# Block inverse of the recurrence in 32x32 tiles, and each direction's sequence over two periods with two chains interleaved

## The chip, the cores and the metric

One Trainium2 chip, one of its cores, float32 throughout. The metric is device time in microseconds (us) of the one launch. Before the change the median of three runs is 3419.12 us (3416.22 to 3426.52).

## The reference, cut to what matters

The program is one layer of a hybrid trunk for a context group (128 positions) and a latent group (512 positions), D = 2048. The change touches one of its parts, the bidirectional RWKV-7 recurrence: 16 heads of width 64, two directions, and per head a 64x64 state that is carried through all positions.

```
def wkv_scan(r, w, k, v, a, b, s0, reverse):
    def step(S, xs):
        r_t, w_t, k_t, v_t, a_t, b_t = xs
        sa = jnp.einsum('bhvk,bhk->bhv', S, a_t)
        S = S * w_t[:, :, None, :] + sa[..., None] * b_t[:, :, None, :] + v_t[..., None] * k_t[:, :, None, :]
        return S, jnp.einsum('bhvk,bhk->bhv', S, r_t)
...
for d, (s0, rev) in enumerate(((s0_f, False), (s0_b, True))):
    ...   # decay, a_rate, k_d of direction d
    o_d, s_d = wkv_scan(..., -kk, kk * a_h, s0, rev)
```

The outputs of both directions are added. Around it lie the input projection, attention, gating, the output projection and an expert layer, none of which changes.

## The kernel before, in words

`block_rwkv` (L1066 to L1590) handles a pair of heads at a time (`NPAIR` = 8, the two heads on partitions 0-63 and 64-127) and for each pair both directions `d`. That makes 16 *periods* (`u = 2p + d`). The 640 positions are `NCK` = 10 chunks of `CK` = 64, two of the context and eight latent.

Per period the kernel prepares one direction and at the same time runs the sequence of the direction prepared in the period before. Everything is written out by hand in a list, `timeline` (L1093 to L1101): 60 *jobs*, and between them the 30 *stages* of the sequence, about one stage after every two jobs. PE, ScalarE (ACT) and VectorE (DVE) each walk the same list in order; a semaphore wait holds all that stands behind it on its engine.

The jobs (`run_job`, L1299) write a rotating set of six PSUM banks (`rot`), and `empty` on ACT (L1406) or DVE (L1499) takes the result out:

- `bk` (3), `vt` (2): products with the identity that turn k, b and v to token order; emptied by ACT.
- `sc` (5): 64x64 by 128 products, two chunks in a job; DVE masks them (L1505).
- `w`, `a` (two halves each) and `s0`: decay and rate of the *next* direction, emptied by ACT with Sigmoid; then the scan on DVE (L1520), six vector operations on GpSimd (POOL; `front`, L1222, and `scaled_r`, L1239), three Exp on ACT (L1435 to L1437) and three products on DVE (L1529, L1534).
- `ti` (3), and then five levels of `x`, `dt`, `dtt` (three batches of 4, 3 and 3 chunks): the inverse of a 64x64 unit triangular matrix per chunk and head by doubling, from blocks of 1 to blocks of 64. POOL starts it (L1253, L1255). Level by level `x` multiplies by the triangular matrix `sc`, DVE masks (L1512), `dtt` and `dt` update the inverse `tt` and its transpose `tm` (L1515). Both are kept since a matmul takes its left side transposed.

All these matmuls go head by head through `heads` (L1286), as 64x64 tiles of the array; only `w` and `a` use 64x128 tiles (L1297). A float32 matmul is two LDWEIGHTS and two MATMUL instructions in the trace.

The sequence (`stage`, L1350 for PE) has three stages per chunk. `pw` issues five products (ten matmuls over the two heads) and needs the state `st`; ACT copies `wsb`. `u` multiplies by `tt`; ACT copies `usb`. `z` issues two products; DVE adds the state (L1553) and scales it (L1559), which releases the next chunk's `pw`. One chain of 10 chunks is thus done within each period, and the last one alone after the last period (L1390).

Before the first period POOL builds masks, one operation at a time (`Chain.link`, L1195 to L1216), and DVE waits for the end of that (L1496).

Of the kernel before, what the change touches and what calls it, by code (L numbers as in the profile page):

```python
# [7 lines left out]

# [1057 lines left out]
def block_rwkv(nc, z_d, kk_d, par_d, w2, a2, state, ident_d, o_raw_d, state_out):  # L1066
# [3 lines left out]
    LEVELS = [2, 4, 8, 16, 32]  # L1070
    BATCH = [(0, 4), (4, 7), (7, 10)]
    HALF = T // 2
    R = 6
    ORDER = [list(range(NCK)), list(range(NCP))[::-1] + list(range(NCP, NCK))[::-1]]
    HEADS = (slice(0, DH), slice(DH, P))
    FRONT_JOBS = [("w", 0), ("a", 0), ("s0", 0), ("w", 1), ("a", 1)]
    FRONT = len(FRONT_JOBS)
# [8 lines left out]
    NJ = len(plan)  # L1086
    assert NJ % R == 0, NJ
    on_act = [j[0] in ("w", "a", "s0", "vt", "bk", "ti") for j in plan]
    NA, ND = sum(on_act), NJ - sum(on_act)
    index = {j: n for n, j in enumerate(plan)}  # L1090


    stages = [(i, s) for i in range(NCK) for s in ("pw", "u", "z")]  # L1093
    LAST = NJ - 6
    timeline = []
    placed = 0
    for n in range(NJ):
        timeline.append(("job", n))
        while placed < len(stages) and placed * LAST < (n + 1) * len(stages):
            timeline.append(("seq", *stages[placed]))  # L1100
            placed += 1  # L1101
    FRONT_END = index[("a", 1)]
    SCAN_AT, EXP_AT, VCOPY_AT = ("job", FRONT_END + 4), ("job", FRONT_END + 18), ("job", FRONT_END + 21)
    PAD_B_AT, PAD_K_AT, PAD_A_AT = ("job", FRONT_END + 26), ("job", FRONT_END + 29), ("job", LAST + 1)

    with ExitStack() as ctx:
# [6 lines left out]
        eye, par, pp = sb("eye", [P, DH]), sb("par", [P, 72]), sb("pp", [P, 10])  # L1113
        mask = sb("mask", [P, 2, 2 * CK])
        join = sb("join", [P, 7, CK])
        reset = sb("reset", [P, T])
        xwa = sb("xwa", [P, T])
        wa2 = sb("wa2", [P, 2, P])
# [4 lines left out]
        halves = sb("halves", [P, NCK])  # L1123
        ec = sb("ec", [P, 2, NCK])
        bk = sb("bk", [P, 2 * NCK, CK])
        vc = sb("vc", [P, NCK, CK])
        aq = sb("aq", [P, 2, NCK, 2, CK])
        bktok = sb("bktok", [P, 2, 2 * NCK, DH])
        vtok = sb("vtok", [P, 2, NCK, DH])
# [1204 lines left out]
```

## Time and profile before

| | us |
|---|---|
| median of the runs | 3419.12 |
| the profiled execution | 3412.67 |
| its span | 3410.9 |
| the recurrence block (from 1030 to 1820 in the span) | about 790 |
| PE busy in the span | 2957.4 (87%) |
| DVE busy in the span | 1448.0 (42%) |
| ACT, POOL busy in the span | 564.5 (17%), 377.9 (11%) |

The profile is one execution. A busy PE is one with an instruction somewhere between its start and its modelled end, so it need not be at its peak rate. Slices of the overview are 85 us each; the recurrence covers slices 13 to 22. The period starts can be read from the `rw_st` memset that begins each sequence: the first at 1094.74, the last at 1781.55.

### The profile page before, as it was taken

To read this page: it belongs to the slowest core of one execution; us is meant where nothing else is said; L and a number is where in the kernel's file an instruction comes from. 1 tells how busy PE (TensorE), PEld (TensorE's weight loads), DVE (VectorE), ACT (ScalarE), POOL (GpSimd) and SP (SyncE) were. 2 spreads that over 40 slices of the span, in tenths; PEclk is the share of its full clock that TensorE was granted. 3 is DMA by queue.
4 is the path that set the end of the run, shared out by engine and by line. 5 is a ranking of instruction groups with operands and counts; after the bars stand their busy time and mean duration, and the time that the engine had idled before them with its cause. 6 is when DMAs were issued, how large, how long until landed. Compare 5 with 4: busy or idle time off the path is not lost. (4 is left out here: it accounts for less than half of the span.)

```text
span 3410.9 us, 72845 instructions
## 1 busy us (share of the span) xinstructions
PE 2957.4 (87%) x32237; PEld 1759.9 (52%) x32237; DVE 1448.0 (42%) x2634; ACT 564.5 (17%) x1331; POOL 377.9 (11%) x431
## 2 busy tenths in 40 slices
PE   5899999998595888888884499977999999999993
PEld 1566666665375888888882245442333333323230
DVE  1677577663363665565652311142232232132123
ACT  2100000000352333333332311110000000000001
POOL 0100000000154232322211000000000000000000
PEclk8899999999597999999995799978999999999996
DMA  9565645552451000000005387777999999999997
GB/s 412 195 213 175 208 176 183 208 196 84 143 132 46 24 5 26 26 26 26 25 8 229 138 300 289 276 308 283 395 410 393 412 412 395 399 397 400 408 419 309
DMA packets 224486, 776.86 MB, mean 228 GB/s; under 512 B 55171, under 2 KB 119386, under 8 KB 155635
## 3 DMA queue, kind: packets, MB, share of 16 engines
q1 hardware_dynamic: 212626, 712.26, 54.1%
q0 software_dynamic: 11248, 60.87, 5.9%
q8 instruction: 200, 3.28, 0.4%
q14 instruction: 44, 0.35, 0.0%
q10 hardware_dynamic: 368, 0.10, 0.0%
HBM read 710.98 MB, written 62.18 MB: 227 GB/s over the span
## 5 line engine op out<-in xcount | busy, mean ns | idle before, releaser
L2068 PE MATMUL ex_ps<-experts_ring,ex_xe 128*32 128x512 f32 (+1 forms) x4608 | 674.6, 599 | 49.1 <-DMA experts_ring<-in_w_up 27.6
L2070 PE MATMUL ex_ps<-experts_ring,ex_xe 128*32 128x512 f32 (+1 forms) x1536 | 674.1, 599 | 0.0
L2068 PEld LDWEIGHTS ex_ps<-experts_ring,ex_xe 128*32 128x32 f32 (+1 forms) x4608 | 212.6, 107 | 497.0 <-issue 479.4
L474 DVE SCALAR_TENSOR_TENSOR pj_macc<-pj_mring,head_cond_t,pj_macc 128x1024 f32<-128x1024 f32 x240 | 296.9, 1277 | 184.0 <-DMA pj_mring<-in_w_ada 184.0
L2083 PE MATMUL ex_ps<-experts_ring,ex_hidt 128*32 128x512 f32 (+1 forms) x2304 | 334.3, 594 | 6.9 <-DVE ex_hidt L2150 6.9
L2085 PE MATMUL ex_ps<-experts_ring,ex_hidt 128*32 128x512 f32 (+1 forms) x768 | 333.8, 594 | 0.0
L547 PE MATMUL pj_ps<-head_hT,head_ring_in 128*128 128x320 f32 x1104 | 313.7, 437 | 5.9 <-DVE head_hT L447 3.5
L1866 PE MATMUL om_ps<-experts_ring,om_ot 128*128 128x512 f32 x640 | 287.1, 610 | 15.4 <-DMA om_ot<-scratch_o 15.4
L2172 DVE SCALAR_TENSOR_TENSOR ex_hid<-ex_hid,ex_gcol,ex_ps 80x512 f32<-80x512 f32 x16 | 11.9, 744 | 591.3 <-ACT ex_hid L2115 591.3
L547 PEld LDWEIGHTS pj_ps<-head_hT,head_ring_in 128*128 128x128 f32 x1104 | 211.4, 192 | 96.6 <-DVE head_hT L447 6.3
L2083 PEld LDWEIGHTS ex_ps<-experts_ring,ex_hidt 128*32 128x32 f32 (+1 forms) x2304 | 106.8, 106 | 225.9 <-issue 218.1
L547 PE MATMUL pj_ps<-pj_t,pj_s 128*128 128x320 f32 x736 | 210.3, 439 | 6.0 <-DVE pj_t L453 6.0
L1866 PEld LDWEIGHTS om_ps<-experts_ring,om_ot 128*128 128x128 f32 x640 | 124.5, 196 | 170.0 <-issue 154.4
L547 PEld LDWEIGHTS pj_ps<-pj_t,pj_s 128*128 128x128 f32 x736 | 141.0, 193 | 72.2 <-issue 10.3
L2070 PEld LDWEIGHTS ex_ps<-experts_ring,ex_xe 128*32 128x32 f32 (+1 forms) x1536 | 162.2, 107 | 0.0
L2150 DVE STREAM_TRANSPOSE ex_xe<-experts_h2t 32x512 f32<-32x512 f32 x192 | 134.7, 702 | 16.9 <-PEq L1743 8.4
L1289 PE MATMUL rw_rot<-rw_tt,rw_xm 64*64 64x64 f32 x3200 | 134.9, 219 | 4.9 <-DVE rw_xm L1512 4.9
L2037 POOL DMA_INDIRECT scratch_ffn<-ex_y,experts_tok x16 | 23.1, 1445 | 991.7 <-ACT ex_y L2126 991.7
L1289 PE MATMUL rw_rot<-rw_tm,rw_sc 64*64 64x64 f32 x3200 | 132.5, 223 | 0.2 <-DVE rw_tm L1515 0.2
L2115 ACT ACTIVATE ex_hid<-ex_ps 80x512 f32<-80x512 f32 x32 | 17.2, 588 | 673.7 <-PE ex_ps L2070 673.7
L432 ACT COPY pj_stage<-pj_ps 128x320 f32<-128x320 f32 x23 | 9.8, 425 | 683.9 <-PE pj_ps L547 683.9
L1289 PEld LDWEIGHTS rw_rot<-rw_tt,rw_xm 64*64 64x64 f32 x3200 | 114.8, 135 | 7.0 <-DVE rw_xm L1512 7.0
(357 smaller groups left out, 4417.4 us busy)
## 6 DMA issues: line engine op xcount, KB each, us to landing
experts_ring<-in_w_gate SPq DMA_DIRECT2D x128, 1024.0 KB, 21.9
experts_ring<-in_w_up SPq DMA_DIRECT2D x128, 1024.0 KB, 22.6
experts_ring<-in_w_down SPq DMA_DIRECT2D x128, 1024.0 KB, 21.3
experts_ring<-in_w_out SPq DMA_DIRECT2D x68, 1024.0 KB, 6.9
pj_mring<-in_w_ada SPq DMA_DIRECT2D x64, 1024.0 KB, 9.0
head_ring_in<-in_w_in SPq DMA_DIRECT2D x23, 2048.0 KB, 8.0
ada_ring<-in_w_ada SPq DMA_DIRECT2D x16, 2048.0 KB, 19.0
scratch_z<-pj_stage POOLq DMA_DIRECT2D x19, 640.0 KB, 8.2
```

What stands on the lines that cost most here:

```text
L474: a = nc.vector.scalar_tensor_tensor(acc, w, scalar, acc, ALU.mult, ALU.add)
L547: mm = pe.matmul(bank(name, b)[:, 0:TH], a[:, k, :], h[:, k, :], start=(k == 0), stop=(k == KH - 1))
L1289: mm = pe.matmul(out[rows], lhs[rows], rhs[rows], start=start, stop=stop, **kw)
L1866: mm = pe.matmul(ps[:, banks(t) + h, :], ot[:, t % 2, k, :], w[:, h * 512:(h + 1) * 512], start=(k == 0), stop=(k == KD - 1))
L2037: pool.indirect_dma_start(out=ffn_rows, out_offset=bass.IndirectOffsetOnAxis(ap=tok[:, e:e + 1], axis=0), in_=y[:], in_offset=None, comput ...
L2068: pe.matmul(ps[rows, bank, :], xe[:, k, rows], cols, start=(k == 0), stop=(k == KD - 1))
L2070: mm = pe.matmul(ps[96:96 + rows.stop - rows.start, bank, :], xe[:, k, rows], up[:, g1], start=(k == 0), stop=(k == KD - 1))
L2083: pe.matmul(ps[rows, 3 + c, :], hidt[:, k, rows], w[:, c * 512:(c + 1) * 512], start=(k == 0), stop=(k == 7))
L2085: mm = pe.matmul(ps[96:96 + rows.stop - rows.start, 3 + c, :], hidt[:, k, rows], w[:, 3 * 512:4 * 512], start=(k == 0), stop=(k == 7))
L2115: nc.scalar.activation(hid[0:M, h * 512:(h + 1) * 512], ps[0:M, 2 * h, :], ACT.Silu).then_inc(silu_done, 1)
L2150: tr = nc.vector.transpose(dst[32 * q:32 * q + 32, :, 32 * g:32 * g + 32], src(g, q))
L2172: nc.vector.scalar_tensor_tensor(half, half, gcol[:], up1[:] if h else ps[0:M, 1, :], ALU.mult, ALU.mult).then_inc(hid_done, 1)
```

## The change

The inverse of a 64x64 block is made on the 32x32 diagonal blocks first (levels 0 to 3), four partition groups at once, and a last level (4) makes the off-diagonal 32x32 block, whose matmuls read one group and write its neighbour. Only one product (`d`) updates the inverse; its transpose now comes from a DVE 32x32 transpose (`turn`) after each `d`. The ten chunks go in two batches of five. The sequence of a direction runs over two periods, so in a period the second half of chain `u-2` and the first half of chain `u-1` alternate stage by stage. `rot` has four banks instead of six, `wu` and `zo` two instead of one.

```diff
-    plan = [("bk", b) for b in range(3)] + [("vt", b) for b in range(2)] + [("sc", b) for b in range(NCK // 2)]
-    plan += FRONT_JOBS + [("ti", b) for b in range(3)]
-    for level in range(len(LEVELS)):
-        plan += [("x", b, level) for b in range(3)]
-        for b in range(3):
-            plan += [("dt", b, level)] if level < len(LEVELS) - 1 else []
-            plan += [("dtt", b, level)]
+        items = [("sc", 0, u), fr[0], ("sc", 1, u), fr[1], ("sc", 2, u), fr[2], ("sc", 3, u), fr[3], ("sc", 4, u)]
+        items += ["scan"] if more else []
+        fill = [("bk", 0, u), ("bk", 1, u), ("bk", 2, u), fr[4], vt[0], vt[1]]
+        for lv in range(LAST_LV + 1):
+            for b in range(2):
+                items += (["turn%d" % b] if lv == 0 else []) + [("x", b, lv, u)]
+            if lv < 3:
+                items.append(fill[2 * lv])
+            for b in range(2):
+                items.append(("d", b, lv, u))
+                if more and lv == 3:
+                    items.append(("exp_in", "exp_inv")[b])
+                if more and lv == 4:
+                    items += (["pad_b"], ["pad_k", "pad_a"])[b]
+            if lv < 3:
+                items.append(fill[2 * lv + 1])
+            if more and lv == 3:
+                items += ["exp_ex", "decay"]
...
+        old, new = chain(u - 2, BC, NCK), chain(u - 1, 0, BC)
+        return [s for pair in itertools.zip_longest(old, new) for s in pair if s is not None]
...   # timeline(u): a stage is placed after every 1/30 of the summed COST of the jobs
+            def start(u, b):                                        # POOL, waits for the sc jobs of batch b
+                nc.gpsimd.tensor_tensor(part[:], lt, first[:].unsqueeze(1).to_broadcast([P, BC, 2, HB]), ALU.mult).then_inc(tinit, 1)
+                nc.gpsimd.tensor_tensor(chunks(tt, b), part[:, :, 0, :], part[:, :, 1, :], ALU.add).then_inc(tinit, 1)
+                nc.gpsimd.tensor_tensor(chunks(tt, b), chunks(tt, b), eye32[:].unsqueeze(1).to_broadcast([P, BC, HB]), ALU.add).then_inc(tinit, 1)
...   # PE, jobs x and d
+                    for i in range(BC):
+                        for g, rows in enumerate(GROUPS):
+                            at = GROUPS[g ^ 1] if last else rows
+                            if kind == "x":
+                                lhs, rhs = sc[rows, u % NS, c, 0, HB * h:HB * h + HB], tm[rows, c, :]
+                            else:
+                                lhs, rhs = xm[rows, c, :], tt[rows, c, :]
+                            mm = pe.matmul(out[at], lhs, rhs, start=True, stop=True)
...   # DVE, job d below the last level, and turn
+                    nc.vector.tensor_tensor(chunks(tt, b), src, chunks(tt, b), ALU.add).then_inc(dve_ev, 1)
+                    dve.wait_ge(dve_ev, RANK[G[key]])
+                    turn(u, b)
+            def turn(u, b):
+                nc.vector.transpose(chunks(tm, b)..., chunks(tt, b)...).then_inc(turned, 1)
...   # DVE, state of the next chunk; ecp is the product of two decays, made on POOL
-                    nc.vector.tensor_scalar(st[:], tmp[:], ec[:, d, c:c + 1], ec[:, d, nx:nx + 1], ALU.mult, ALU.mult).then_inc(s_ready, 1)
+                    nc.vector.tensor_tensor(st[:, k, :], tmp[:, k, :], ecp[:, r, c:c + 1].to_broadcast([P, DH]), ALU.mult).then_inc(s_ready[k], 1)
...   # POOL, masks before the first period: 68 chained operations (MADE) instead of 43
+            for i in range(5):
+                for rows in GROUPS:          # was: 6 levels for each of the two halves
```

In the new order `sc` stands first in a period and needs all three `pad_` products of its direction, which now stand at the very end of the period before. The last level's `x` is emptied by ACT, behind the Exp operations in ACT's order. POOL further writes the diagonal blocks into `tw` (`spread_own`) and multiplies neighbouring decays (`decay_pairs`). The copy of the values (`copy_values`, L1442) is gone. SP loads the next pair's rows at a later point, as soon as the last readers of the old ones are done, and the small weights one pair further ahead. After the 16 periods two short lines follow: in the first the second half of chain 14 alternates with the first half of chain 15, in the second the rest of chain 15 runs alone.

## Rows read from the trace of the kernel before

**Rows 1.** The page: busy time by engine, and the 40 slices.

```profile
PE 2957.4 (87%) x32237; PEld 1759.9 (52%) x32237; DVE 1448.0 (42%) x2634; ACT 564.5 (17%) x1331; POOL 377.9 (11%) x431
PE   5899999998595888888884499977999999999993
```

**Rows 2.** Busy time by stretch: stretch, us, busy (instructions) by engine, clock, DMA share, GB/s.

```profile
1062.40:1094.74 32.34, 30.62 (x833) 28.82 (x832) 21.79 (x53) 9.64 (x18) 12.20 (x13) 0.95 0.03 6
1781.55:1817.40 35.85, 23.67 (x324) 18.54 (x324) 5.28 (x22) 6.47 (x31) 0.53 (x1) 0.56 0.01 2
1094.74:1781.55 686.81, 607.82 (x17020) 567.90 (x17014) 410.45 (x1089) 236.82 (x753) 189.43 (x195) 0.98 0.07 23
```

**Rows 3.** PE's order of time: start us, us, x instructions; a `bk` job and what follows, then five `sc` jobs.

```profile
1234.10 1.10 PE L1289 MATMUL rw_rot<-rw_eye,rw_bk 64*64 64x64 f32 x32
1235.04 0.28 PE L1289 MATMUL rw_wu<-rw_wsb,rw_tt 64*64 64x64 f32 x4
...
1066.98 4.55 PE L1289 MATMUL rw_rot<-rw_aq,rw_bk 64*64 64x128 f32 x80
```

**Rows 4.** PE's order of time around the 64x128 jobs `w` and `a`.

```profile
1336.89 0.31 PE L1289 MATMUL rw_zo<-rw_aq,rw_st 64*64 64x64 f32 x4
1337.13 0.80 PE L1297 MATMUL rw_rot<-rw_xwa,rw_wa 64*128 64x320 f32 x2
1337.86 0.33 PE L1289 MATMUL rw_rot<-rw_eye,rw_sin 64*64 64x64 f32 x4
1338.03 0.28 PE L1289 MATMUL rw_wu<-rw_wsb,rw_tt 64*64 64x64 f32 x4
1338.24 0.81 PE L1297 MATMUL rw_rot<-rw_xwa,rw_wa 64*128 64x320 f32 x4
1338.98 0.33 PE L1289 MATMUL rw_zo<-rw_usb,rw_bktok 64*64 64x64 f32 x4
```

**Rows 5.** Who waited for whom in 1094.74 to 1781.55: total us, times, longest.

```profile
PE rw_zo L1289 <- DVE rw_tmp L1553: 26.8, 36, 1.0
PE rw_wu L1289 <- ACT rw_wsb L1452: 25.9, 14, 1.9
PE rw_wu L1289 <- DVE rw_fs L1557: 13.6, 14, 1.0
```

**Rows 6.** DVE's groups by form, 1094.74 to 1781.55: count, busy us, mean ns, idle before.

```profile
L1515 DVE TENSOR_TENSOR rw_tt<-rw_rot,rw_tt 128x192 f32<-128x192 f32 x150 | 53.0, 354 | 47.8 <-PE rw_rot L1289 43.4
L1559 DVE TENSOR_SCALAR rw_st<-rw_tmp,rw_ec 128x64 f32<-128x64 f32 x120 | 52.2, 435 | 4.4
L1505 DVE TENSOR_TENSOR rw_sc<-rw_rot,rw_mask 128x512 f32<-128x512 f32 x75 | 51.8, 691 | 35.1 <-PE rw_rot L1289 35.1
L1515 DVE TENSOR_TENSOR rw_tt<-rw_rot,rw_tt 128x256 f32<-128x256 f32 x75 | 31.4, 419 | 19.4 <-PE rw_rot L1289 19.4
L1520 DVE TENSOR_TENSOR_SCAN rw_cs<-rw_reset,rw_sg 128x640 f32<-128x640 f32 x14 | 20.7, 1480 | 0.0
L1534 DVE SCALAR_TENSOR_TENSOR rw_aq<-rw_kk,rw_e_ex 128x640 f32<-128x640 f32 x14 | 12.5, 895 | 0.0
L1529 DVE TENSOR_TENSOR rw_bk<-rw_kd,rw_e_inv 128x640 f32<-128x640 f32 x14 | 11.4, 813 | 0.0
```

**Rows 7.** The page's groups: the transposes that DVE makes in the expert layer.

```profile
L2150 DVE STREAM_TRANSPOSE ex_xe<-experts_h2t 32x512 f32<-32x512 f32 x192 | 134.7, 702 | 16.9 <-PEq L1743 8.4
```

**Rows 8.** ACT's groups, 1088 to 1820: table load, Exp.

```profile
L1435 ACT ACT_TABLE_LOAD x14 | 18.0, 1283 | 0.2
L1435 ACT ACTIVATE rw_e_in<-rw_pq 128x640 f32<-128x640 f32 x7 | 5.2, 737 | 0.1
```

**Rows 9.** POOL and DVE before the first period, in order of time.

```profile
1034.68 0.65 POOL L1211 TENSOR_SCALAR_AFFINE_SELECT rw_join<-rw_join 64x64 f32<-64x64 f32 x1
1044.83 0.24 POOL L1213 TENSOR_SCALAR_AFFINE_SELECT rw_join<-rw_join 64x64 f32<-64x64 f32 x1
1047.60 0.17 DVE L1538 COPY rw_pp<-rw_par 128x9 f32<-128x9 f32 x1 [22.28 <-POOLq L1217]
```

More of the change, by code:

```diff
@@ L1093, in block_rwkv @@
[L1093 to L1104, printed above, removed]
+    GROUPS = tuple(slice(HB * g, HB * g + HB) for g in range(4))
@@ L1219, in _ @@
-            for s in (o_ev, z_ev, u_ev, osum_done, o_out, fo_out):
-                pool.sem_inc(s, 1)
-            def front(u, first=False):
-                pool.wait_ge(cs_done, u + 1)
-                if not first:
-                    pool.wait_ge(ec_done, u)
-                    pool.wait_ge(pad_done, u)
+            for g, rows in enumerate(GROUPS):
+                for h in range(2):
+                    ch.link(nc.gpsimd.memset(half[rows, h:h + 1], 1.0 if h == g % 2 else 0.0))
+            for h in range(2):
+                ch.link(nc.gpsimd.tensor_scalar(first[:, h, :], join[:, 0, :], half[:, h:h + 1], None, ALU.mult))
@@ new lines, in _ @@
+            pool.wait_ge(once_in, 8 * 16)
+            front(0)
+            scaled_r(0)
+            decay_pairs(0)
+            added = 0
+            for u in range(NU):
+                for b in range(2):
+                    start(u, b)
+                if u + 1 < NU:
+                    front(u + 1)
+                    scaled_r(u + 1)
+                for b in range(2):
+                    spread_own(u, b)
+                if u + 1 < NU:
+                    decay_pairs(u + 1)
+                if u % 2 == 0 and u // 2 >= CHAINS:
+                    add_directions(added)
+                    added += 1
@@ L1379, in period @@
-            def period(p, d, first, last):
-                for item in timeline:
-                    if item[0] == "job":
-                        run_job(item[1], p, d, first, last)
-                    elif not first:
-                        stage(item[1], item[2], 2 * p + d - 1, 1 - d)
-            pe.wait_ge(loads, NLOAD)
-            for n, (kind, half) in enumerate(FRONT_JOBS):
-                front_job(kind, half, 0, rot[:, n]).then_inc(job, 1)
-            periods(period)
-            for i, s in stages:
-                stage(i, s, 2 * NPAIR - 1, 1)
+                    pe.wait_ge(w_ev[k], q + 1)
@@ new lines, in _ @@
+            for key in front_jobs(0):
+                empty(key)
+            for which in ("exp_in", "exp_inv", "exp_ex"):
+                exponential(which, 0)
+            chunk_decays(0)
+            for u, line in enumerate(LINES):
+                for item in line:
+                    if item[0] == "seq":
+                        stage(*item[1:])
+                    elif item in ("exp_in", "exp_inv", "exp_ex"):
+                        exponential(item, u + 1)
+                    elif item == "decay":
+                        chunk_decays(u + 1)
+                    elif not isinstance(item, str) and on_act(item):
+                        empty(item)
```

626 lines of the change are left out of this document (319 added, 307 removed).

## The prediction

> **What bounds the kernel now.** I read the overview first: PE is the busiest engine, 2957.4 us of the span [rows 1]. Its slices tell the stages apart. The change touches only the recurrence, so I cut that stretch by the starts of its sequences and asked for busy time by stretch [rows 2]. From the second period to the last sequence there are 15 periods in 686.81 us, 45.8 us each. The first period, which has no sequence in it, takes 32.34 us. The last sequence, which has nothing beside it, takes 35.85 us. PE is busy for 607.82 of the 686.81 us at a clock of 0.98; DVE for 410, ACT for 237, POOL for 189. The reader should see that PE's order of work sets the period and that no other engine comes near. As the difference between a period with a sequence and one without, 13.5 us is what a sequence costs PE's queue.
>
> A busy PE is not a full PE, so I take the rate from the starts. 32 instructions of a job begin at 1234.10 and the next group at 1235.04: 0.94 us, 29 ns each [rows 3]. Five `sc` jobs (80 instructions, twice the columns) take 4.48 us to the next start, 56 ns each [rows 3]. A 64x128 job has two instructions that last 0.80 us, some 0.53 us of queue.
>
> One period before, in MATMULs: inversion 10 chunks x 2 heads x 2 instructions x (5 `x` + 5 `dtt` + 4 `dt` + 1 `ti`) = 600, at 29 ns 17.4 us. The sequence, 324, 9.4 us. `bk`, `vt`, `s0`: 80, 20 (as a mean) and 4, 3.0 us. `sc` 80, 4.5 us. `w`, `a` 2.1 us. Sum 36.4 us. The other 9.4 us are waits and gaps. The waits shown are those on DVE's state sum, on ACT's `wsb` and on `fs`: 26.8 + 25.9 + 13.6 = 66 us, 4.4 us per period [rows 5]; the rest is changes of tile form (below), short waits and the fill of the pipeline.
>
> **Inversion in 32x32 tiles.** Removed: those 600 MATMULs. Added: 5 levels x (`x`, `d`) x 10 chunks x 4 groups x 2 = 800, each with its LDWEIGHTS, each half as many columns. The trace has no 32x32 tile. From above: the nearest form costs 29 ns, and a smaller tile should not cost more, 23.2 us. From below: a tile's 64 columns take 58 ns for the two heads that run side by side; half the columns and four groups side by side give 29 ns / 4 = 7.3 ns, 5.8 us. That groups do run side by side is seen at 1338.24: four 64x128 instructions (`w` and `a`, on different halves of the rows) last 0.81 us, two alone 0.80 us [rows 4]. I take 12 ns, 9.6 us. It is nearer the lower end because of that row, and above it because two instructions must be issued for each 12 ns, where the fastest run shown issues two in 29 ns. Both ends stay in the range: one nanosecond is worth 0.8 us per period, 12.8 us in the whole.
>
> The Trainium skill (page "TensorE: Matmul & The Clock Gate", section "Back-to-back issue gap") has a floor of about 25 ns from start to start for 1 to 64 columns; by it the inversion would cost 800 x 25 = 20 us. Part 3 of that page lets matmuls of different tiles start some 4 ns apart, which speaks for the lower end. The equal times at 1338.24 [rows 4] bear out the second and do not show a floor between tiles; at the rate of the queue neither is tested here.
>
> **Changes of tile form.** The new order switches between 64x64 and 32x32 tiles at every stage of the sequence. The trace shows such a change around the 64x128 jobs [rows 4]. From 1336.89 four instructions should take 0.12 us, the next begins after 0.24. From 1337.13 two take 0.53, the next begins after 0.73. Then 0.21 for 0.12, and 0.74 for 0.53. Extra: 0.12, 0.20, 0.09, 0.21, on average 0.15 us. Counting along the new list, a full period has 44 to 46 changes, where the old one has 6. That is 6.8 us instead of 0.9 us. The lower bound is nothing where the engine waits anyway; the upper is 0.21 each, 9.5 us.
>
> **The other PE work** stays: 9.4 + 3.0 + 4.5 + 2.1 = 19.0 us.
>
> **The sequence over two periods.** Each chain now has only 15 stages in a period and the other chain's stage lies between two of its own. A copy by ACT or a sum by DVE has at least one job and one foreign stage to hide behind. So I take the 4.4 us of waits [rows 5] as gone. Doing the state scaling as a plain product (about 0.22 us instead of a mean of 435 ns [rows 6]) is off the path in full periods.
>
> **What is late next.** Three places of the new order hold PE.
> (a) `sc` opens a period and needs `pad_a`, the last DVE work of the one before. After the last `d` jobs DVE still has two evictions (0.35 each), the sums and scalings of two chains (0.9), two `bk` products at 0.81 and `pad_a` at 0.90 [rows 6], about 4.1 us, against 1.6 us of PE's own work. 2.5 us.
> (b) The first `x` needs `turn0`, which stands behind the last `sc` mask (0.69) and the scan (1.48) on DVE [rows 6]. A transpose of 160 elements should cost 0.33, since one of 512 takes 702 ns [rows 7] and a step of 64 elements costs 65 ns [rows 6]. With signals 2.8 us, against 0.75 us of PE work after the last `sc`. 2.1 us. POOL's start of the second batch ends about then too.
> (c) ACT's table load and the three Exp, 1.28 + 3 x 0.73 [rows 8], a decay and a copy stand ahead of the last level's first eviction: 4.2 us against some 2.4 us of PE work. 1.8 us.
> With half a microsecond for the turns between levels, 7 us. From below 4 (the queue evens them out), from above 12 (each of the five levels waits another microsecond for mask, sum and transpose).
>
> **The sum.** A full period: 19.0 + 9.6 + 6.8 + 7.0 = 42.4 us, 3.4 us less than 45.8.
> - 14 full periods (the third to the sixteenth): -48 us.
> - Second period, half a sequence: 42.4 - 4.7 (162 instructions) - 1.9 (some 13 changes fewer) = 35.8 instead of 45.5: -10 us.
> - First period, no sequence: 42.4 - 9.4 - 3.6 = 29.4 instead of 32.3: -3 us.
> - After the periods: two short lines. One chunk alone takes 35.85 / 10 = 3.6 us [rows 2]. Five alternating pairs take about 3.6 us each, as a pair has only 72 instructions, 2.1 us at 29 ns; then five alone take 18 us. 36 us: unchanged (bounds -4 and +4).
> - Before the first period DVE waits for POOL's masks, 22.28 us, ended by POOL [rows 9]. The chain grows by 25 operations. An affine select takes 0.65 to 0.24 us plus 0.07 us for the link [rows 9]; on half the columns I take 0.25 us per added operation. +6 us.
> Sum -55 us. The profiled execution takes 3412.67 us for a span of 3410.9; it would come to 3358. The median is 6.5 us above it, so I forecast 3419 - 55 = 3364 us. The DMA-bound stages behind begin that much earlier and do not change. The loads of the next pair move, but they still have most of a period to land, and SP's queue holds nothing else that is urgent.
>
> **Rivals.**
> 1. *Tiles side by side to the full, waits evened out.* 8 ns per instruction and 4 us of waits: 19.0 + 6.4 + 6.8 + 4 = 36.2 us a period, 6.2 less than my forecast, x 15: 3364 - 93 = 3271 us. For it: the equal 0.80 and 0.81 us [rows 4]. Against it: no run of instructions comes faster than 29 ns.
> 2. *Slower: the queue's issue rate decides.* If a pair of LDWEIGHTS and MATMUL can't be issued in less than about 25 ns, 800 of them take 20 us. Some waits vanish under it (5 left): 50.8 us a period, 5 us more than before, and some 8.4 more than forecast, x 16: 3364 + 134 = 3498 us. It decides from 12 + 55 / 12.8 = 16 ns on: above that the change loses. For it: 600 MATMULs become 800, and no run in the trace is faster than 29 ns. Against it: that 29 ns equals what the tiles' columns alone account for, two heads at a time. The floor of the Trainium skill named above would give just this case.
> 3. *Slower: the levels wait for each other.* One level is matmul, mask, matmul, sum, transpose, over three engines with only two batches to overlap and four banks. With 12 us of waits the period is 47.4 us: 3364 + 5 x 16 = 3444 us. For it: DVE's evictions already show 43.4 us of idle on PE for one group [rows 6], so the two run close. Against it: each level has some 5 us of PE work, and one batch's round trip is about 2.5 us.
> 4. *The clock.* The last sequence, with little PE work, runs at 0.56, the periods at 0.98 [rows 2]. If the small tiles with their gaps let the clock fall to its lower level (1.2 instead of 2.4 GHz) for a quarter of the time, a quarter of 16 x 35 us of PE work doubles: +140 us, 3504 us. Against it: PE stays in work all through.
>
> **Chances.** Forecast 0.42 (its own range 3325 to 3405), rival 1 0.18, rival 2 0.18, rival 3 0.15, rival 4 0.07. This kernel's measurement can tell about 0.3% (10 us) from no change. Faster: nearly all of the first two and a little of the third, 0.61; same 0.05; slower 0.34. The range for 8 in 10 runs from rival 1's centre to rival 2's: 3265 to 3495 us.
>
> **What would show it.** Periods of about 42 us between the `rw_st` memsets of one parity; `x` and `d` jobs of 40 instructions in about 0.5 us with a gap of 0.15 us at each change of form; the first `sc` of a period waiting 2 to 3 us for DVE (`pad_a`), the first `x` some 2 us for a transpose, the first `d` of the last level for ACT; waits for `wsb` and the state sum near nothing; the masks 6 us later. The prediction is wrong if the 40 instructions take over 0.65 us, if the clock in the periods is below 0.9, or if levels wait for DVE by more than a microsecond each.

## The result: slower, and what the profile after shows

| | before | after |
|---|---|---|
| median of the runs, us | 3419.67 (3416.22 to 3426.52) | 3546.64 (3536.72 to 3565.61) |
| profiled execution's span, us | 3410.9 | 3534.9 |
| one of 13 periods (second to fifteenth `rw_st` memset), us | 46.2 | 53.7 |

The ratio is 1.0375 (95% interval 1.0321 to 1.043). The forecast was 3364 us with a range of 3265 to 3495: wrong in sign, and the time lies outside the range. The runs behind the two medians were made for this comparison; the later batches give 3411 to 3418 us for the kernel before.

The page after, against [rows 1]; the last two rows are the granted clock by slice and the queue that brings the engines' instructions (200 packets before):

```profile
PE 2979.2 (84%) x35105; PEld 1732.0 (49%) x35105; DVE 1356.3 (38%) x2410; ACT 551.2 (16%) x1286; POOL 419.4 (12%) x504
PE   5899999996767778777777369995999999999993
PEclk8899999998685877787787689997999999999996
q8 instruction: 224, 3.67, 0.4%
```

PE has more instructions, is busy for a smaller share in the recurrence (slices of 7 where there were 8), and the clock there, 0.98 before [rows 2], reads 5 to 8. By stretch, first the kernel before over the same 13 periods, then the kernel after: the first period from its scan on, the second, 13 periods, the last, and the short lines behind.

```profile
1049.92:1094.74 44.82, 31.29 (x840) 29.51 (x842) 26.46 (x57) 13.00 (x23) 20.57 (x20) 0.83 0.02 4
1140.22:1741.09 600.87, 529.26 (x14776) 494.36 (x14774) 359.68 (x950) 207.92 (x656) 173.32 (x176) 0.98 0.07 22
```

```profile
1056.92:1123.21 66.29, 40.31 (x1058) 31.73 (x1058) 22.28 (x45) 15.21 (x26) 23.96 (x24) 0.55 0.07 24
1123.21:1175.80 52.59, 40.14 (x1156) 33.25 (x1156) 18.19 (x50) 12.64 (x33) 14.88 (x16) 0.65 0.02 4
1175.80:1873.71 697.91, 552.76 (x17126) 470.69 (x17126) 287.41 (x767) 196.94 (x623) 202.72 (x214) 0.79 0.06 20
1873.71:1911.81 38.10, 31.43 (x1220) 28.04 (x1220) 15.96 (x53) 7.98 (x35) 6.72 (x9) 0.87 0.02 4
1911.81:1945.90 34.09, 24.13 (x484) 19.68 (x484) 6.30 (x31) 9.67 (x47) 1.53 (x1) 0.79 0.04 14
```

The 13 periods hold 97.0 us of the difference (697.91 - 600.87), the first stretch 21.5, the second 7.1 (52.6 against 45.5 before), the start of the scan 7.0 (the masks, forecast 6). The end gives back 4; the span grew by 124.0. The memset stands later in the new order: PE does 5.9 us of a period's work ahead of it, where it did 0.8, so some 5 us of the first stretch belong to the second period.

PE's order of time after, in a stretch at the upper clock; in brackets the idle time before a row and what ended it:

```profile
1190.57 1.02 PE L1420 MATMUL rw_rot<-rw_tt,rw_xm 32*32 32x32 f32 x80
1191.52 0.33 PE L1368 MATMUL rw_zo<-rw_usb,rw_bktok 64*64 64x64 f32 x4
...
1193.20 0.28 PE L1368 MATMUL rw_zo<-rw_aq,rw_st 64*64 64x64 f32 x4
1193.42 0.44 PE L1420 MATMUL rw_rot<-rw_tm,rw_sc 32*32 32x32 f32 x29
1194.70 0.31 PE L1420 MATMUL rw_rot<-rw_tm,rw_sc 32*32 32x32 f32 x11 [0.84 <-issue]
1194.96 0.33 PE L1368 MATMUL rw_wu<-rw_eye,rw_fs 64*64 64x64 f32 x4
1195.10 0.31 PE L1368 MATMUL rw_zo<-rw_vtok,rw_bktok 64*64 64x64 f32 x4
1195.22 0.31 PE L1368 MATMUL rw_zo<-rw_sc,rw_vtok 64*64 64x64 f32 x4
1195.34 0.31 PE L1368 MATMUL rw_wu<-rw_vtok,rw_sc 64*64 64x64 f32 x4
1195.45 0.31 PE L1368 MATMUL rw_wu<-rw_st,rw_aq 64*64 64x64 f32 x4
1195.57 0.31 PE L1368 MATMUL rw_zo<-rw_aq,rw_st 64*64 64x64 f32 x4
1195.81 0.55 PE L1420 MATMUL rw_rot<-rw_tm,rw_sc 32*32 32x32 f32 x40
1196.29 0.33 PE L1368 MATMUL rw_wu<-rw_wsb,rw_tw 64*64 64x64 f32 x4
1196.46 0.63 PE L1368 MATMUL rw_rot<-rw_eye,rw_bk 64*64 64x64 f32 x16
1196.92 0.28 PE L1368 MATMUL rw_wu<-rw_wsb,rw_tw 64*64 64x64 f32 x4
1197.14 0.43 PE L1420 MATMUL rw_rot<-rw_tt,rw_xm 32*32 32x32 f32 x27
1198.55 0.32 PE L1420 MATMUL rw_rot<-rw_tt,rw_xm 32*32 32x32 f32 x13 [0.98 <-issue]
```

Two things are to be seen. 80 instructions in 32x32 tiles take 0.95 us to the next start, 11.9 ns each: my 12 ns. But inside a job PE stops for 0.84 and 0.98 us, with nothing in the profile to wait for. Add up the MATMULs from 1194.70 to the next stop: 11 + 6 x 4 + 40 + 4 + 16 + 4 + 27 = 126, with a LDWEIGHTS each 252, and with the four semaphore instructions that the trace has between them 256. The stops before and after it (1197.38, 1201.09, 1204.62, 1208.74 as the last start ahead of each) lie exactly 256 PE instructions apart too. The DMA view of 1190 to 1203, in 40 slices of 0.325 us (only instruction queues moved anything; the last packet, the 25, is one of 8 KB on another queue):

```profile
GB/s 0 0 0 0 0 0 50 0 0 0 0 0 0 0 0 0 0 0 0 50 0 0 0 0 0 0 0 0 0 50 0 0 0 0 0 0 0 25 0 0
q8 instruction: 3, 0.05, 1.5%
```

Three packets of 16 KB on q8, 64 bytes for each of 256 instructions (a *page*), start at about 1192.2, 1196.2 and 1199.6 us and take about 1 us each (1.5% of 16 engines in 13 us is 3.1 us for three); PE goes on some 1.4 us after each has landed. The same holds for all 60 stops of the 13 periods: each ends 1.2 to 1.6 us after such a packet has landed, while the waits for other engines end anywhere between two packets. Where two stops lie one page apart, PE went through the page in 3.3 to 4.2 us, median 3.7 us (40 cases). That is 14.4 ns per instruction and 29 ns for a pair of LDWEIGHTS and MATMUL, about the pitch of the old 64x64 jobs [rows 3]. Jobs at 11.9 ns per pair outrun the pages and stand still at their end.

Who PE waited for in those 13 periods (total us, times, longest), against [rows 5]:

```profile
PE rw_rot L1420 <- issue: 42.9, 42, 1.9
PE rw_rot L1420 <- DVE rw_tm L1557: 39.4, 26, 1.8
PE rw_rot L1368 <- DVE rw_aq L1593: 34.1, 13, 3.7
PE rw_zo L1368 <- issue: 7.6, 7, 2.1
PE rw_rot L1368 <- issue: 5.5, 6, 1.2
PE rw_wu L1368 <- DVE rw_st L1617: 5.5, 10, 0.7
PE rw_wu L1368 <- issue: 4.9, 5, 1.5
PE rw_wu L1368 <- DVE rw_st L1607: 4.4, 13, 0.5
PE rw_rot L1420 <- ACT rw_xm L1492: 0.6, 2, 0.3
```

The "issue" rows are the stops: 60.9 us, 4.7 per period. The others come to 84.0 us, 6.5 per period. The view counts a wait from the modelled end of the last MATMUL; from its start to the next start the stops are 5.6 us and the others 7.6 us per period.

The Trainium skill (page "Runtime: NRT & Kernel Launch", section "Instruction fetch mechanics") says that instructions come in 16 KiB blocks of 256 and that crossing a block is mostly hidden, since issue is slower than the refill. The 256 agree with the count above; that it is mostly hidden holds for the 64x64 jobs, but not for the 32x32 jobs here, with 60 stops in 13 periods.

### The profile page after: what moved, and what is told of

It reads as the page before. It is cut to its first block and busy times, and to the rows that moved or that the text cites. A ratio compares the mean times of both kernels' runs of the same rounds, so it can differ in the third digit from the quotient of the medians.

```text
span 3534.9 us, 78594 instructions
## 1 busy us (share of the span) xinstructions
PE 2979.2 (84%) x35105; PEld 1732.0 (49%) x35105; DVE 1356.3 (38%) x2410; ACT 551.2 (16%) x1286; POOL 419.4 (12%) x504
## 3 DMA queue, kind: packets, MB, share of 16 engines
q1 hardware_dynamic: 212818, 712.28, 52.1%
## 5 line engine op out<-in xcount | busy, mean ns | idle before, releaser
L1920 PE MATMUL om_ps<-experts_ring,om_ot 128*128 128x512 f32 x640 | 287.5, 611 | 15.2 <-DMA om_ot<-scratch_o 15.2
L2226 DVE SCALAR_TENSOR_TENSOR ex_hid<-ex_hid,ex_gcol,ex_ps 80x512 f32<-80x512 f32 x16 | 11.9, 744 | 586.8 <-ACT ex_hid L2169 586.8
L1368 PE MATMUL rw_rot<-rw_aq,rw_bk 64*64 64x128 f32 x1280 | 123.9, 353 | 51.9 <-DVE rw_aq L1593 51.9
L1420 PE MATMUL rw_rot<-rw_tm,rw_sc 32*32 32x32 f32 x6400 | 103.3, 208 | 76.0 <-DVE rw_tm L1557 48.2
L1368 PEld LDWEIGHTS rw_rot<-rw_aq,rw_bk 64*64 64x64 f32 x1280 | 100.5, 181 | 74.5 <-issue 70.2
L1420 PE MATMUL rw_rot<-rw_tt,rw_xm 32*32 32x32 f32 x6400 | 104.3, 209 | 32.5 <-issue 31.5
L1420 PEld LDWEIGHTS rw_rot<-rw_tm,rw_sc 32*32 32x32 f32 x6400 | 82.0, 119 | 93.5 <-DVE rw_tm L1557 54.1
## 6 DMA issues: line engine op xcount, KB each, us to landing
experts_ring<-in_w_down SPq DMA_DIRECT2D x128, 1024.0 KB, 22.6
```

The source lines that it names most:

```text
L1368: mm = pe.matmul(out[rows], lhs[rows], rhs[rows], start=start, stop=stop, **kw)
L1420: mm = pe.matmul(out[at], lhs, rhs, start=True, stop=True)
L1920: mm = pe.matmul(ps[:, banks(t) + h, :], ot[:, t % 2, k, :], w[:, h * 512:(h + 1) * 512], start=(k == 0), stop=(k == KD - 1))
L2226: nc.vector.scalar_tensor_tensor(half, half, gcol[:], up1[:] if h else ps[0:M, 1, :], ALU.mult, ALU.mult).then_inc(hid_done, 1)
```

## The experiments

All are edits of the kernel after, each timed beside the kernel before; as the batches differ by a few us, two versions are best compared by their ratios. wide2, wide5 and warm5 leave out part of the inverse (the products with some chunks' own left sides), so their results are not the reference's; all others compute everything. "Stops" are the issue rows and "waits" the other rows of PE's waits, per period, over the same 13 periods as above; "clock" is the mean granted clock in them. Some expectations put the stops of the kernel after at 6.65 to 6.8 us and those of wide5 at 0.85; the table's figures are those of the view.

| | us | ratio to before (95%) | period | clock | stops | waits |
|---|---|---|---|---|---|---|
| before | 3419.67 | | 46.2 | 0.98 | 0.05 | 5.4 |
| after | 3546.64 | 1.0375 (1.0321 to 1.043) | 53.7 | 0.79 | 4.7 | 6.5 |
| wide2 | 3421.61 | 1.0012 (0.9988 to 1.0036) | 46.0 | 0.86 | 0.7 | 8.0 |
| wide5 | 3414.98 | 0.9984 (0.9963 to 1.0004) | 46.6 | 0.82 | 0 | 8.4 |
| oldinv_two_chains | 3300.11 | 0.9648 (0.9617 to 0.9678) | 38.5 | 1.00 | 0 | 0.8 |
| chain1 | 3609.9 | 1.057 (1.0527 to 1.0614) | 57.9 | 0.74 | 4.5 | 7.8 |
| clump | 3552.34 | 1.0371 (1.033 to 1.0412) | 53.3 | 0.79 | 5.7 | 6.4 |
| split | 3540.17 | 1.0368 (1.0333 to 1.0403) | 53.9 | 1.00 | 0.3 | 0 |
| warm | 3485.01 | 1.0213 (1.0186 to 1.024) | 49.8 | 0.89 | 5.8 | 2.5 |
| warm5 | 3330.78 | 0.9754 (0.9729 to 0.978) | 40.8 | 0.96 | 0 | 4.1 |
| cols | 3528.5 | 1.0353 (1.0319 to 1.0387) | 52.1 | 0.90 | 4.4 | 5.8 |
| cols_warm | 3477.06 | 1.0179 (1.0146 to 1.0212) | 49.6 | 0.99 | 5.2 | 2.4 |
| bkfirst | 3484.29 | 1.0193 (1.0152 to 1.0234) | 50.9 | 0.81 | 4.4 | 6.0 |

In every version but chain1 and before, each single stop (448 with those of after) ends 1.2 to 1.6 us after the landing of a 16 KB instruction packet. In chain1 this is so for 56 of 95, 3.7 of the 4.5 us; the other 39 are short.

**Fewer instructions, the same columns: wide2 and wide5.** Theory A: the number of PE instructions sets the pace. B: tile forms or levels do.

```diff
-                    for i in range(BC):
+                    for i in range(0, BC, W):          # W = 2, 5
+                        m = min(W, BC - i)
-                        out = bank[:, i * HB:(i + 1) * HB]
+                        out = bank[:, i * HB:(i + m) * HB]
-    ... tm[rows, c, :]
+    ... tm[rows, c:c + m, :].rearrange("p c k -> p (c k)")   # tt likewise
```

> The changed kernel, but each x and d matmul takes the moving columns of two chunks at once (64 instead of 32), so that a job has 24 instead of 40 MATMULs; the same columns go through the array, the tile changes, the jobs, all evictions and waits stay. Left out: the products with the second chunk's own left side. Theory A (instructions arrive too slowly: in the trace of the changed kernel PE stands still about 1 us every 256 LDWEIGHTS and MATMULs, 6.8 us per period): instructions per period fall from about 2700 to 2080, pages of 256 from 10.4 to 8.1, the stops from 6.8 to under 1.5 us, about 3547 - 16 x 5.5 = 3460 us. Theory B (changes of tile form and waits for other engines made the loss): nothing of that changes, 3547 us within 1%. Theory C (the lower clock, 44% of the time, is a thing of its own): clock share unchanged, at most 20 us less.

> As wide2, with the moving columns of all five chunks (160) in one matmul: 8 MATMULs in a job. Left out: the products with the own left sides of four chunks in five. Theory A: 5.6 pages per period, no stops at page ends at all; below what wide2 gives by little, since wide2 should already be free of most stops: 3430 to 3460 us. If the cost went with the number of instructions without a threshold, it would fall again as much as for wide2, to about 3370. Theory B: 3547 us within 1%.

Measured: 3421.61 and 3414.98 us, both under A's figures. Dropping 16 of 40 MATMULs per job, with all their columns kept, takes 7.7 us from the period, and 0.7 of the 4.7 us of stops are left; the rest of the gain, which makes it larger than A had it, goes with the clock (0.79 to 0.86), which theory C had unchanged. Dropping 16 more takes out the rest of the stops and gains nothing further: once they are gone something else sets the period. The waits have grown to 8 us and the clock is still low:

```profile
1152.90:1758.40 605.50, 495.20 (x8806) 366.12 (x8806) 286.71 (x767) 195.02 (x623) 209.59 (x214) 0.82 0.06 21
PE rw_rot L1421 <- DVE rw_tm L1558: 41.3, 32, 1.8
PE rw_rot L1368 <- DVE rw_aq L1594: 40.1, 13, 3.7
PE rw_rot L1421 <- ACT rw_xm L1493: 15.8, 13, 1.2
```

(wide5, its 13 periods and its longest waits.) So A holds for the stops, and a second cause is left.

**One part at a time: oldinv_two_chains and chain1.** With before and after they make a square: old or new inverse, one or two chains. It is not a clean one. The new inverse brings its order of jobs with it (`sc` first, the `pad_` products last; see bkfirst), and the corner "old inverse, one chain" is the kernel before, which also has six banks instead of four, fewer buffers for `aq` and the other order of loads. Only the two pairs in the new frame (after with chain1, after with oldinv_two_chains) differ in one of the two alone.

```diff
 # oldinv_two_chains, in the frame of the kernel after
+    LEVELS = [2, 4, 8, 16, 32]
+    items += [("ti", b, u) for b in range(3)]
+    for level in range(len(LEVELS)):
+        items += [("x", b, level, u) for b in range(3)]
+        for b in range(3):
+            items += [("dt", b, level, u)] if level < len(LEVELS) - 1 else []
+            items += [("dtt", b, level, u)]
 # chain1
-    CHAINS = 2
+    CHAINS = 1
```

> The other half of the change alone: the old inverse in 64x64 tiles (600 MATMULs, transposes by matmul, three batches), in the changed kernel's frame: each direction's sequence over two periods, two chains alternating, four rotating banks, the product of two decays from GpSimd. The whole computation is done. Theory A: 8.8 pages per period as before the change, no page stops, no added tile changes, and the sequence's 4.4 us of waits per period gone: about 3419 - 50 = 3370 us. Rival (the two-chain sequence with fewer banks is itself what loses): 3480 us or more.

> The whole change but one part: the new inverse in 32x32 tiles with one chain per period instead of two (the fourth corner of old or new inverse x one or two chains; the other three stand at 3418, 3300 and 3547 us). A (two separate causes that add: the inverse costs, the two chains gain): the two chains gave 7.7 us per period with the old inverse, from waits of the sequence that they filled (4.4 by the waits of before, and the rest from the work placed in them); with the new inverse one chain has these waits back, but the stops of about 1 us every 256 instructions fall into some of them: 55 to 61 us per period, 3580 to 3660 us. B (the two chains themselves hurt beside the new inverse, by changes of tile form and by scattering the 32x32 jobs): at or below 3547 us.

Measured: 3300.11 and 3609.9 us. The two chains gain 7.7 us per period with the old inverse and 4.3 with the new one; the new inverse with its order costs 11.7 us with one chain and 15.2 with two. Two causes of opposite sign, that add in sign though not exactly in size. A has both directions; chain1 is within its range, oldinv_two_chains is 70 us faster than A had it, since I had priced the two chains by the wait rows alone. What is left of waits in oldinv_two_chains, in all 13 periods:

```profile
1132.60:1632.80 500.20, 489.47 (x14538) 465.14 (x14534) 338.51 (x948) 196.47 (x639) 170.74 (x188) 1.00 0.09 27
PE rw_wu L1346 <- ACT rw_wsb L1491: 6.5, 13, 0.6
PE rw_rot L1346 <- DVE rw_xm L1542: 3.8, 6, 0.6
```

This version computes everything and is faster than both kernels.

**Fewer changes of tile form: clump.** The first-half `x` and `d` jobs are followed at once by the second-half ones, without a stage of the sequence between them: 34 changes per period instead of 45, counted in the traces (the expectation has 28).

```diff
+            if i[0] in ("x", "d") and i[1] == 0:
+                continue
             while placed < len(seq) and (placed + 1) * total <= spent * len(seq):
```

> The changed kernel, but no stage of the sequence stands between the two x jobs or the two d jobs of a level, only after them: about 28 instead of 45 changes of tile form in a period, with the same instructions. Theory B (changes of form cost 0.15 us each on the path): 17 x 0.15 x 16 = 40 us less, 3505 us. Theory A (the arrival of instructions sets the pace, so a shorter change only makes PE reach the end of its page sooner): 3547 us within 0.5%.

Measured: 3552.34 us, no gain (the interval reaches over after's). The stops grew from 4.7 to 5.7 us per period: the 32x32 jobs stand closer together, and run into the page's end together. What fewer form changes could give (11 at some 0.075 us, by the price found below), the stops took; that the one turned into the other is not shown.

**The same columns in more instructions: split.** The converse, in the fast version without 32x32 tiles.

```diff
-                        mm = heads(bank[:, i * CK:(i + 1) * CK], lhs, rhs, True, True)
+                        for h in range(2):
+                            mm = heads(bank[:, i * CK + h * HB:i * CK + h * HB + HB],
+                                       lhs, rhs[:, h * HB:h * HB + HB], True, True)
```

> The kernel with the old 64x64 inverse and two chains (3300 us, 38.5 us per period, 8.9 pages of 256 TensorE instructions per period, no stops), with each inverse product split by its columns into two matmuls of 32 columns: same result and same columns, 560 LDWEIGHTS and MATMUL pairs or 4.4 pages more per period. A (TensorE can't go through a page of 256 instructions in under about 3.65 us): 13.2 pages take at least 48 us; stops of about 1 us reappear every 256 instructions, 5 or more per period, time 3455 to 3540 us. B (the stops belong to the 32x32 tiles): no stops; only the array's own time for the added matmuls, which isn't over 20 ns each or 11 us per period: 3300 to 3470 us, and no gap of 1 us at multiples of 256.

Measured: 3540.17 us, which neither theory has right. A's time is met at its edge but its stops are missing (0.3 us per period). B's missing stops are met, but 560 pairs cost 15.4 us a period, 27.5 ns each, not under 20. The order of time of split shows the same pitch for half the columns:

```profile
1332.88 1.07 PE L1346 MATMUL rw_rot<-rw_tm,rw_sc 64*64 64x32 f32 x32
1333.79 0.31 PE L1346 MATMUL rw_zo<-rw_usb,rw_bktok 64*64 64x64 f32 x4
```

0.91 us for 32, 28 ns each, where 64 columns took 29 [rows 3]. So in the 64x64 form the pair has a price of its own, whatever its columns, and at 28 ns it only just keeps pace with the pages (13.1 pages of 256 in 53.9 us, 4.1 us each). Only 4 stops came in 13 periods, so it doesn't show that 64x64 jobs can be made to stop as the 32x32 ones do. The Trainium skill (page "TensorE: Matmul & The Clock Gate", section "LDWEIGHTS (loading the stationary operand)") makes a weight load cost its columns over 1.2 GHz; for 64 columns that is an estimate of 53 ns, 27 ns if two heads load side by side, and these rows agree with it. The 32x32 jobs do not: the same estimate would give them 7 ns with four groups, and they took 11.9.

**The clock: warm and warm5.** Dummy matmuls, 32 MATMULs over 256 columns per period, fill the three long waits, in the kernel after and in wide5.

```diff
                 before = [JOBS[g - R]] if g >= R else []
+                warm = {("sc", 0): 4, ("x", 0): 3, ("x", 1): 1}.get((kind, b), 0) if u and (kind == "sc" or key[2:3] == (0,)) else 0
+                if warm:
+                    emptied(before)
+                for _ in range(warm):
+                    heads(bank[:, 0:256], eye[:], reset[:, 0:256], True, True)
```

> The changed kernel with 4, 3 and 1 pairs of 64x64 matmuls on 256 columns put ahead of the three waits in which TensorE stands longest in each period (the first score job, and the first inverse job of either half), their result overwritten. It computes all that the kernel computes. 16 matmuls more per period, 0.13 of a page of 256 instructions. The clock stands at the lower level in 42% of the periods' time. A (the waits pull the clock down and its lower level is a cost of its own): the share falls under 25% and with it 1 to 4 us per period: 3485 to 3535 us. B (the stops every 256 instructions set both pace and clock, the waits matter little): clock share stays at 35% or more, time 3540 to 3570 us.

> As warm, but in the kernel whose inverse jobs have 8 matmuls on 160 columns instead of 40 on 32 (wide5: all but one chunk's left operands of each five are left out, so its inverse is not the reference's; 3415 us, 46.6 us per period, clock at the lower level in 37% of it, 0.85 stops per period). There the stops are nearly gone and the waits for Vector are what is left. A (clock held down by the waits): the share of the lower level falls under 15% and the period by 3 to 6 us: 3320 to 3370 us. B (the dummy work only delays, the clock falls for another reason): 3410 to 3440 us.

Measured: 3485.01 and 3330.78 us, A in both (the first at the very edge of its range). Work that computes nothing gained 62 and 84 us, 55 and 79 us by the ratios. The share of the periods' time at the lower level (1.2 GHz) fell from 42 to 22% and from 37 to 8%. The windows of warm and of warm5:

```profile
1163.30:1810.90 647.60, 540.01 (x17542) 442.20 (x17542) 278.38 (x768) 197.15 (x623) 202.73 (x214) 0.89 0.07 21
```

```profile
1146.30:1676.50 530.20, 475.07 (x9222) 336.04 (x9222) 273.33 (x768) 193.94 (x623) 208.76 (x214) 0.96 0.08 24
```

With neither stops nor much time at the low clock the small-tile inverse, here with 160 wide MATMULs for its 800, has a period of 40.8 us, near the forecast's 42.4. The stretch ahead of the 13 periods took 12 us less in warm as well.

**Stops and clock apart: cols and cols_warm.** 640 of the 800 inverse matmuls run over twice the columns.

```diff
-                        out = bank[:, i * HB:(i + 1) * HB]
+                        w = 2 if i < BC - 1 else 1
+                        out = bank[:, i * HB:(i + w) * HB]
-    ... tm[rows, c, :]
+    ... tm[rows, c:c + w, :].rearrange("p c k -> p (c k)")   # tt likewise
```

> The changed kernel, its 800 inverse matmuls per period the same in number, but 640 of them run over 64 columns instead of 32 (the second half is overwritten by the next matmul; nothing is left out). A job of 24 such matmuls in wide2 took 0.42 us, which makes some 20 ns of one with 64 columns against 11.9 ns with 32: 640 x 8.4 ns = 5.4 us more of array time per period, 86 us over 16 periods. A (the pace is set by the pages of 256 instructions, and the short matmuls only run ahead and then stop): the added columns go into the stops, which shrink by 3 us or more per period from 6.65; the period grows by 0 to 2.5 us, time 3545 to 3590 us. B (array time and stops add): stops stay at 6 us or more and the period grows by 5 us: 3620 us or more.

> cols and warm together: 640 of the 800 inverse matmuls over 64 columns, and 4, 3 and 1 pairs of dummy matmuls ahead of the long waits; it computes all that the kernel computes. A (the clock's cost is gone with warm plus wider matmuls, the pages' stops stay): share of the lower level under 8%, period 46 to 49 us, stops of 4 us or more per period by the waits view: 3425 to 3475 us, still not faster than before. B (the stops come from the clock or from short matmuls, not from the pages): stops under 2 us per period and a time under 3420 us.

Measured: 3528.5 us for cols. 80% more columns in the inverse did not make the kernel slower, which lies outside both expectations. Whether it became faster is not clear: the 18 us are within the two intervals, though the profiled period is shorter too (52.1 for 53.7 us). It is not for A's reason: the stops hardly shrank (4.4 us). The clock made up for the columns: its lower level's share went from 42 to 19%, with nearly the same waits (5.8 for 6.5 us). cols_warm runs its 13 periods at 0.99 and still stops:

```profile
1165.40:1810.10 644.70, 544.60 (x17542) 451.35 (x17542) 276.88 (x768) 196.57 (x623) 202.48 (x214) 0.99 0.07 21
PE rw_rot L1426 <- issue: 49.0, 63, 1.4
```

3477.06 us, two microseconds above A's range; A's share, period (49.59, at its upper end) and stops hold, B is out. The stops don't come from the clock, nor only from the shortest matmuls. That the new inverse would lose at the full clock too is not shown by this: cols_warm runs some 5.4 us of added columns and 3.6 us of dummy work in each period.

**Real work in the waits: bkfirst.**

```diff
-        items = [("sc", 0, u), fr[0], ("sc", 1, u), ...
+        items = [("bk", 0, u), ("bk", 1, u), ("sc", 0, u), fr[0], ("sc", 1, u), ... ("sc", 4, u), ("bk", 2, u)]
-        fill = [("bk", 0, u), ("bk", 1, u), ("bk", 2, u), fr[4], vt[0], vt[1]]
+        fill = [None, None, None, fr[4], vt[0], vt[1]]
```

> The changed kernel with real work in place of warm's dummy matmuls: two of the three bk jobs (some 0.9 us each) open the period ahead of the first score job, the third stands behind the last score job, ahead of the first inverse job; they no longer stand between the levels. Same instructions, another order. A (it is the long waits at the turn of the period that pull the clock down): the wait for the last DVE product falls from 2.6 to about 1 us per period and that for the first transpose by about 0.5 us; the share of the lower clock falls from 42% to 25 to 35% and the period by 2 to 4 us: 3485 to 3515 us. B (only keeping the array full helps, the order doesn't, or the levels now wait where bk stood): 3530 us or more, clock as before.

Measured: 3484.29 us, A's time, but its clock only in part: the share of the lower level is 38%, and the waits fell only from 6.5 to 6.0 us: the one for the last DVE product from 2.6 to 1.6 us, but the one for the transposes rose from 3.0 to 4.2 us. Over the 13 periods it gained 37 us (53.7 to 50.9 each), the rest ahead of them. The order of real work is worth as much as the dummy work here. Stops and waits account for 0.8 of the 2.8 us per period; the time at the lower level fell from 22.6 to 19.3 us per period, and as half the clock can at most double the time of a piece of work, that is worth up to 1.6 us. So most of the gain can lie in the clock; that it does is not shown. It also means that part of what the square puts down to the new inverse is its order of jobs.

## Why the prediction was wrong

**The step that failed first: "I take 12 ns, 9.6 us"**, the price of 800 MATMULs. As a pitch it was right (11.9 ns). As a price it was not: it counted what a tile takes and not what the instruction stream can bring. The stops add 4.7 us per period to the 9.5 (wide5 and oldinv_two_chains have none), so a MATMUL costs 17.8 ns, beyond the 16 ns that the prediction names as the point of no gain. Rival 2 was the right mechanism in the mean, with the wrong form: not every pair is slow, but every 256th instruction stops. Its argument against itself (29 ns is what the columns account for) hid that 29 ns per pair is also about the pages' own pace (median 3.7 us for 256): the old kernel's dense stretches sat at that pace and showed next to nothing of it (0.05 us of stops per period).

**The step that failed most: the clock, "PE stays in work all through"** (rival 4, chance 0.07). With measured terms, and the prediction's 19.0 us for the other work, a period is 19.0 + 9.5 + 4.0 (form changes, below) + 4.7 + 6.5 = 43.7 us. It took 53.7. The 10.0 us over are a rest and not a measured term, but they fit the clock: 22.6 us of each period are spent at the lower level, and half the clock can cost at most half of that, 11.3 us. The same sum for the other versions, in us per period; the last column is half the time at the lower level, the most that the clock can have cost:

| | other work + inverse + form changes + stops + waits | sum | measured | clock | at most |
|---|---|---|---|---|---|
| after | 19.0 + 9.5 + 4.0 + 4.7 + 6.5 | 43.7 | 53.7 | 0.79 | 11.3 |
| oldinv_two_chains | 19.0 + 17.4 + 0.9 + 0 + 0.8 | 38.1 | 38.5 | 1.00 | 0 |
| cols_warm | 19.0 + 14.9 + 4.0 + 5.2 + 2.4 + 3.6 dummy work | 49.1 | 49.6 | 0.99 | 0.4 |
| cols | 19.0 + 14.9 + 4.0 + 4.4 + 5.8 | 48.1 | 52.1 | 0.90 | 5.0 |
| wide5 | 19.0 + 8.0 + 4.0 + 0 + 8.4 | 39.4 | 46.6 | 0.82 | 8.6 |

(cols has 9.5 + 5.4 for the added columns, wide5 160 matmuls at 50 ns, the dummy work 32 MATMULs over 256 columns at twice the 56 ns of 128 columns.) The sum fits within 0.5 us where the clock is full and misses by 4 to 10 us where it isn't, each time by less than the clock can have cost. Of the gap, warm and warm5 gave back 3.9 and 5.8 us per period by dummy work alone. The sum is good to some 3 us: with stops and waits counted from start to start it would be 45.8 us for after and 52.0 for cols_warm, 2.4 more than measured. By either count the stops alone would not have made the kernel slower (43.7 or 45.8 us against 46.2 before), and the clock made it so. That is an estimate; no run has the new inverse in full with its clock held and nothing added.

**The waits** were sized right, 6.5 us for 7, and (a) 34.1 / 13 = 2.6 us for 2.5. (b) was 3.0 with both halves for 2.1. (c) is nearly nothing (0.6 us in all); in wide2 and wide5, where the stops are few or gone, it is there with 0.8 and 1.2 us per period, so it is likely the stops that give ACT its time. What such waits may do to the clock was not priced.

**Changes of tile form** cost little more than half of what I took. 1193.20 to 1193.42 is 0.22 for 0.12 us of work, 1196.29 to 1196.46 is 0.17 for 0.12, and going back after the 40 at 1195.81 takes nothing beyond them: 0.15 for a pair of changes, not for each. Of the 45 changes in a period 37 are to or from 32x32 tiles, 2.8 us; the other 8, to and from 64x128, keep the old 0.15 each [rows 4], 1.2 us. That makes 4.0 us instead of 6.8.

**The two chains** gained more than the 4.4 us: 7.7 per period with the old inverse. The wait rows account for 4.6 (5.4 to 0.8). Counted from start to start the same waits shrink from 7.0 to 1.1 us, 5.9, since the modelled end of a MATMUL covers the beginning of each wait. The clock's last 4% at the lower level are worth at most 0.9 us, and about 1 us stays unexplained.

**First and last periods.** The first was forecast to shorten by 3 us. From PE's first job behind the scan to the first job of the next period it grew from 32.2 to 47.7 us (1061.74 to 1093.94 before, 1069.60 to 1117.28 after), at a granted clock of 0.50 in its first 17 us and 0.61 in the next 30, with 7.2 us of stops and some 6 us of waits for DVE. The wait of 13.4 us for `rw_aq` ahead of it is no part of the loss: before, PE waited there for 17.5 us. The pages are seen most plainly in this period, one stop every 3.6 to 4.0 us, each 256 PE instructions behind the one before:

```profile
1099.64 0.92 PE L1420 MATMUL rw_rot<-rw_tm,rw_sc 32*32 32x32 f32 x76 [1.63 <-issue]
1103.65 0.90 PE L1420 MATMUL rw_rot<-rw_tt,rw_xm 32*32 32x32 f32 x50 [1.98 <-issue]
1107.22 0.52 PE L1420 MATMUL rw_rot<-rw_tm,rw_sc 32*32 32x32 f32 x21 [0.48 <-issue]
1110.81 0.97 PE L1420 MATMUL rw_rot<-rw_tm,rw_sc 32*32 32x32 f32 x56 [1.16 <-issue]
1114.77 0.37 PE L1420 MATMUL rw_rot<-rw_tt,rw_xm 32*32 32x32 f32 x10 [1.92 <-issue]
```

The tail of 36 us took 34.1, the masks 7 us for 6.

**The range** missed because rivals 2 and 4 were priced as if only one could come. Rival 2's period was 50.8 us, rival 4 would have added to it; they came together.

**Open.** That the stops are the arrival of instruction pages rests on their spacing of 256, on the fixed 1.2 to 1.6 us between a packet's landing and the end of each stop, and on wide2 and wide5; no run changed the fetch itself. Why the old kernel held its clock with 5.4 us of waits per period and the new one lost it with 6.5 is not settled: the new waits are fewer and longer (3.7 against 1.9 us), and warm fits that. But cols raised the clock to 0.90 with the waits nearly as they were, and the time that PE stands, stops and waits together, does not order the versions either (7.6 us at 0.99 in cols_warm, 8.4 at 0.82 in wide5). So long waits are at most a part of it.

## What to carry to other kernels

Count the instructions of the busiest engine beside its array time: here dense stretches of TensorE work took 3.3 to 4.2 us for 256 instructions, so a change that swapped 600 matmuls at 29 ns (17.4 us) for 800 at 12 ns (9.5 us) paid 14.2 us with the stops. Look at the granted clock after a change as well: work that got shorter but left more of a period at the lower level lost here. When "issue" heads the waits of an engine, count instructions between the stops. Separate a change's parts before judging it: spreading the sequence over two periods, with its buffers, was worth 3.5% alone, and the block inverse it came with, in its order of jobs, cost over twice that.

## What the runs showed of the hardware that I had not expected

- TensorE stopped at page ends when pairs of LDWEIGHTS and MATMUL came every 12 or 20 ns: 60 stops of up to 2.1 us in 13 periods, one every 3.6 to 4.0 us in the first, each ending 1.2 to 1.6 us after a 16 KB instruction packet had landed. At 28 to 29 ns per pair there were 0 to 4 in 13 periods (before, oldinv_two_chains, split).
- Four 32x32 tiles side by side start a MATMUL of 32 columns every 11.9 ns; a pair in the 64x64 form costs 28 to 29 ns with 32 or 64 columns.
- Adding work made a kernel faster: 32 dummy MATMULs per period gained some 55 to 62 us; 80% more inverse columns cost nothing. In both the lower clock level's share was about halved.
- A DVE transpose of 128x160 in 32x32 blocks took 343 ns (forecast 330):

```profile
L1557 DVE STREAM_TRANSPOSE rw_tm<-rw_tt 128x160 f32<-128x160 f32 x130 | 44.6, 343 | 12.3 <-POOL rw_tt L1318 8.8
```
